# First two seven-product pairs of each FFN: own room and early loads for their weights; RMSNorm factors spread by a column

## The chip, the cores and the metric

One core of one Trainium2 chip runs the whole program. The metric is the time of one execution on the device, in microseconds (us); the median of three runs is compared.

## What is computed

One decoder layer over 520 tokens (8 tokens of running samples and a prompt of 512), model width 1024: a half-step SwiGLU FFN (hidden width 2816), a mixer (retention beside an SSD scan), cross attention over 256 memory tokens, and a second half-step FFN. Every sub-layer starts with an RMSNorm. The parts that the change touches, cut from the reference:

```python
def rmsnorm(x, gain):
    xf = x.astype(jnp.float32)
    y = xf * lax.rsqrt(jnp.mean(xf * xf, axis=-1, keepdims=True) + EPS)
    return (y * gain.astype(jnp.float32)).astype(x.dtype)

def swiglu(x, w1, w3, w2):
    return (jax.nn.silu(x @ w1) * (x @ w3)) @ w2
...
h = x + (0.5 * swiglu(rmsnorm(x, p['ffn1_norm']), p['ffn1_w1'], p['ffn1_w3'], p['ffn1_w2'])).astype(x.dtype)
```

## The kernel before

**Products.** All activations lie feature-major: 128 partitions, a tile per 128 features, 520 token columns taken as two halves of 260. Every matrix product is made in three passes on split operands (`three`: lines 472, 473, 474), hi and lo parts of weights and activations. ScalarE makes the hi part of a weight (`w_hi`, line 425 or 453), VectorE subtracts it from the loaded weight and so makes the lo part (`w_lo`, line 435). A unit is 1024 columns of weights: 8 blocks, two halves, three passes, 48 matmuls.

**The up stage of an FFN.** `w1` and `w3` have 22 pairs of tiles. The first 4 pairs (`PLAIN`) go as 8 plain units. The other 18 (`WIN`) go by a Strassen-Winograd scheme with seven products a pair: forms `a11, a12, s2, s1, s3, s4, a22`, in this order, 12 matmuls each. Their activations (`xs_hi`, `xs_lo`, from `blend`) are made by VectorE and ScalarE beside the plain units; `win_pe` waits for all four of `xs_lo` (line 766) before it starts. A pair's weights lie in five quarters of 512 columns: quarter 0 `a11`, 1 `a12`, 3 `a22`, and two sums, quarter 4 (`s1`) and quarter 2 (`s3`). A sum is made by two transfers: SyncE loads one addend, and then GpSimd's queue issues a transfer that adds the other (`sums_pool`, lines 2578 and 2579). VectorE makes two more sums from these (`s2`, `s4`: `sum_dve`, line 727), and hi and lo parts of each form are made by ScalarE (line 708) and VectorE (line 713), six forms ahead of TensorE. Even pairs use `raw_0` and `z1_0`, odd pairs `raw_1`. `raw_0` is also the buffer of the plain units' weights (`w_raw`), and `raw_1` lies over `x_hi` and `x_lo`, which the plain units read. Hence the first two pairs' loads wait:

```python
if i == 0:
    nc.sync.wait_ge(w_lo, up.u0 + up.units)
elif i == 1:
    nc.sync.wait_ge(unit_done, up.u0 + up.units)
```

The first waits until the last plain unit is split, the second until it is multiplied. SyncE's queue, like every engine's program, is strictly in order; so is VectorE's, where the places of the first forms are fixed by hand (`FIRST_FORMS`: forms 0 and 1 at plain unit 5, 2 and 3 at unit 6, 4 and 5 at unit 7). At unit 5 VectorE does form 0's lo part, the sum `s2`, form 1's lo part, and only then the output of unit 6 (line 1087) and the last `xs_lo`. After a pair's third product it adds `join` (line 827), for which TensorE waits one pair later.

**The norms.** ScalarE squares `h` and VectorE adds the squares up in `sq_sum`. `norm_rows_pe` (line 568) sums over partitions into one column per 128 tokens, ScalarE takes the root (line 582), VectorE the reciprocal (line 588) and then a diagonal matrix for each 128 tokens from it (line 590); `norm_spread_pe` (line 597) multiplies ones by these diagonals, which gives every partition the factor of every token, and ScalarE copies that to `rstd` (lines 606, 607). Outputs are scaled by `rstd` as they leave PSUM. This is done for six norms: `ffn1`, `mix`, `mem`, `ssd`, `x`, `ffn2`. In the first unit after a norm starts TensorE multiplies the not yet scaled `h`; for `ffn1` the row sums come in the middle of unit 1 and the spread after unit 1, for `mix`, `x` and `ffn2` the row sums come after unit 0 and the spread after 5 of the 8 blocks of unit 1. The third unit needs the PSUM pair of the first, which VectorE frees only with `rstd` in hand (line 1087 in an FFN, 1219 in the mixer).

## Time and profile before

| what | value |
|---|---|
| median of 3 runs | 1240.49 us (1239.48 to 1240.67) |
| the profiled execution's own time | 1237.87 us |
| its span, first to last instruction | 1236.1 us |
| TensorE busy | 1199.6 us, 97% of the span |
| VectorE busy | 794.7 us, 64% |
| ScalarE busy | 519.3 us, 42% |
| mean granted TensorE clock | 0.996 of full speed |

The profiled execution is one single run, so its span is the sum against which terms are made; it is 2.6 us below the median. TensorE's busy time counts overlapped matmuls once. A row of the timeline with x10 for five matmuls counts the two passes in which the profile shows a 4-byte product that is not split.

### The profile page before, as it was taken

What the parts mean: (1) busy time and instruction counts of PE and PEld (TensorE: products, weight loads), DVE (VectorE), ACT (ScalarE), POOL (GpSimd) and SP (SyncE); (2) the same over time, 40 slices, a digit from 0 to 9 for tenths busy, and PEclk for the clock granted to TensorE, in tenths of its full rate; (3) what the DMA queues carried; (4) which work ended last, traced back from release to release, by engine and by line L of the source; (5) the groups of instructions that cost most, each with busy time, mean ns of one, the idle gap of its engine ahead of it and who ended that gap; (6) DMA issues with size and microseconds to landing.
All of it is one profiled execution on the core that took longest, in us unless ns stands there. A gap on an engine that the chain in (4) does not pass through costs nothing.

```text
span 1236.1 us, 23510 instructions
## 1 busy us (share of the span) xinstructions
PE 1199.6 (97%) x9699; PEld 1146.0 (93%) x9699; DVE 794.7 (64%) x1246; ACT 519.3 (42%) x848; POOL 124.2 (10%) x154
## 2 busy tenths in 40 slices
PE   7999999999999999999888999999999999999997
PEld 7999999999999979999766999679999999999997
DVE  6888888863336618765787542445679888893332
ACT  6445444552223223264864421433435554562221
POOL 0012111000001000043310010200011111100000
PEclk9999999999999999999999999999999999999999
DMA  4388777343323312221575446812168777633322
GB/s 161 110 203 207 182 184 181 98 125 94 90 84 126 104 54 69 69 99 64 185 248 177 135 172 222 324 35 88 66 170 196 186 182 182 165 98 104 94 77 69
DMA packets 64212, 169.47 MB, mean 137 GB/s; under 512 B 7232, under 2 KB 9472, under 8 KB 61680
## 3 DMA queue, kind: packets, MB, share of 16 engines
q1 hardware_dynamic: 47424, 118.22, 30.5%
q0 software_dynamic: 16144, 49.29, 16.3%
q8 instruction: 74, 1.21, 0.4%
q10 hardware_dynamic: 544, 0.53, 0.1%
q14 instruction: 26, 0.21, 0.1%
HBM read 158.96 MB, written 9.06 MB: 136 GB/s over the span
## 4 chain that ended last, share of the span: by engine, by line
PE 86%; DVE 6%; ACT 3%; DMA 3%; issue 2%; SPq 0%; POOL 0%; DVEq 0%; ACTq 0%
PE ps L472 26%; PE ps L473 26%; PE ps L474 26%; DMA raw<-in_w_up 2%; PE ps L2350 1%; PE ps L2288 1%; DVE w_lo L435 1%; ACT w_hi L425 1%; ACT x_hi L613 1%; PE ps L2251 1%; PE ps L1498 1%; PE ps L597 0%; PE ps L2442 0%; DVE sq_sum L552 0%; DMA raw<-in_w_xv 0%
## 5 line engine op out<-in xcount | busy, mean ns | idle before, releaser
L472 PE MATMUL ps<-xs_lo,w_hi 128*128 128x260 f32 x1008 | 284.8, 283 | 5.2 <-DVE xs_lo L766 3.0
L473 PE MATMUL ps<-xs_hi,w_lo 128*128 128x260 f32 x1008 | 285.5, 283 | 0.0
L474 PE MATMUL ps<-xs_hi,w_hi 128*128 128x260 f32 x1008 | 284.9, 283 | 0.0
L435 DVE TENSOR_TENSOR w_lo<-raw,w_hi 128x1024 fp32r<-128x1024 f32 (+1 forms) x132 | 157.5, 1194 | 153.4 <-ACT w_hi L425 147.2
L474 PE MATMUL ps<-x_hi,w_hi 128*128 128x260 f32 (+1 forms) x896 | 253.6, 283 | 0.0
L473 PE MATMUL ps<-x_hi,w_lo 128*128 128x260 f32 (+1 forms) x896 | 253.3, 283 | 0.0
L472 PE MATMUL ps<-x_lo,w_hi 128*128 128x260 f32 (+1 forms) x832 | 241.8, 291 | 6.9 <-DVE x_lo L618 2.3
L425 ACT ACTIVATE w_hi<-raw 128x1024 fp32r<-128x1024 f32 (+1 forms) x128 | 130.8, 1026 | 208.4 <-PE ps L474 169.9
L708 ACT ACTIVATE w_hi<-raw 128x512 fp32r<-128x512 f32 x234 | 139.3, 626 | 170.2 <-DVE raw L727 135.0
L472 PE MATMUL ps<-gu_lo,w_hi 128*128 128x260 f32 x704 | 199.0, 283 | 1.6 <-DVE join L839 1.6
L472 PEld LDWEIGHTS ps<-xs_lo,w_hi 128*128 128x128 f32 x1008 | 190.0, 188 | 6.1 <-DVE xs_lo L766 3.4
L474 PEld LDWEIGHTS ps<-xs_hi,w_hi 128*128 128x128 f32 x1008 | 189.7, 188 | 0.0
L473 PEld LDWEIGHTS ps<-xs_hi,w_lo 128*128 128x128 f32 x1008 | 189.4, 188 | 0.0
L473 PEld LDWEIGHTS ps<-x_hi,w_lo 128*128 128x128 f32 x896 | 169.5, 189 | 2.0 <-issue 1.9
L474 PEld LDWEIGHTS ps<-x_hi,w_hi 128*128 128x128 f32 x896 | 169.5, 189 | 0.0
L472 PEld LDWEIGHTS ps<-x_lo,w_hi 128*128 128x128 f32 x832 | 157.5, 189 | 11.4 <-issue 10.4
L474 PE MATMUL ps<-gu_hi,w_hi 128*128 128x260 f32 x576 | 162.8, 283 | 0.0
L473 PE MATMUL ps<-gu_hi,w_lo 128*128 128x260 f32 x576 | 162.8, 283 | 0.0
L713 DVE TENSOR_TENSOR w_lo<-raw,w_hi 128x512 fp32r<-128x512 f32 x234 | 153.9, 684 | 0.8 <-ACT w_hi L708 0.7
L472 PEld LDWEIGHTS ps<-gu_lo,w_hi 128*128 128x128 f32 x704 | 132.6, 188 | 2.0 <-DVE join L839 2.0
L474 PEld LDWEIGHTS ps<-gu_hi,w_hi 128*128 128x128 f32 x576 | 108.6, 189 | 0.0
L473 PEld LDWEIGHTS ps<-gu_hi,w_lo 128*128 128x128 f32 x576 | 108.2, 188 | 0.0
(373 smaller groups left out, 1767.1 us busy)
## 6 DMA issues: line engine op xcount, KB each, us to landing
raw<-in_w_up SPq DMA_DIRECT2D x162, 256.0 KB, 3.5
raw<-in_w_down SPq DMA_DIRECT2D x32, 512.0 KB, 3.6
raw<-in_w_up POOLq DMA_DIRECT2D x54, 256.0 KB, 5.5
cache<-in_cache POOLq DMA_DIRECT2D x11, 1024.0 KB, 9.2
raw<-in_w_up SPq DMA_DIRECT2D x16, 512.0 KB, 3.5
raw<-in_w_down SPq DMA_DIRECT2D x16, 384.0 KB, 3.1
v_early<-in_cache POOLq DMA_DIRECT2D x5, 1024.0 KB, 9.8
z<-in_w_up SPq DMA_DIRECT2D x18, 256.0 KB, 2.8
```

The source lines that it names most:

```text
L425: nc.scalar.activation(w_hi_t[j][:, 0:cols], w_raw[j % RAW][:, 0:cols], ACT.Copy).then_inc(w_hi, 1)
L435: nc.vector.tensor_tensor(w_lo_t[j][:, 0:cols], w_raw[j % RAW][:, 0:cols], f32(w_hi_t[j][:, 0:cols]), ALU.subtract).then_inc(w_lo, 1)
L472: nc.tensor.matmul(out, w_h, m_l, start=start, stop=False)
L473: nc.tensor.matmul(out, w_l, m_h, start=False, stop=False)
L474: return nc.tensor.matmul(out, w_h, m_h, start=False, stop=stop)
L613: nc.scalar.activation(dest, source, ACT.Copy, scale=gain(name, k)).then_inc(x_hi_done, 1)
L708: nc.scalar.activation(form_slot(w_hi_t, n), form_source(FORMS[n]), ACT.Copy).then_inc(f_hi, 1)
L713: nc.vector.tensor_tensor(form_slot(w_lo_t, n), form_source(FORMS[n]), f32(form_slot(w_hi_t, n)), ALU.subtract).then_inc(f_lo, 1)
L1498: mm = nc.tensor.matmul(bank(6 + a), ones, ssd_au[:, a * BANK:(a + 1) * BANK], start=True, stop=True)
L2251: mm = nc.tensor.matmul(s_row(n, q), qm[:, n, d, q, :], cache[:, n % 3, (q * 2 + d) * MEM:(q * 2 + d + 1) * MEM], start=n == 0 and d == 0, ...
L2288: mm = nc.tensor.matmul(out, qx(2 * i + d)[:, chunk(c)], mem_k[:, 2 * i + d, :], start=d == 0, stop=d == 1)
L2350: mm = nc.tensor.matmul(bank(b), mem_v[:, m, n * P:(n + 1) * P], att[:, i, :], start=m == 0, stop=m == 1)
```

## The change

**Weights of the first two pairs.** `raw_first` is a new tile of five quarters for pair 1, laid over a part of `gu`'s area that nothing holds until later pairs' outputs are written. `first_win_loads` replaces the loads of pairs 0 and 1. The first addends of three sums are issued right behind the last plain unit's load (for the second FFN after a wait for the units before it); quarters 0 and 1 of pair 0 wait for the split of the last but one plain unit, quarter 2 and 3 for the split of the last, and the rest of pair 1 follows with no wait of its own. GpSimd's additions and VectorE's and ScalarE's waits for pair 0 count the first of the two additions alone where only that one is needed (`both_or_first`). Pair 2 waits for pair 0's additions and for `f_hi` of pair 0's `a22`; the wait for the last plain unit's product moves to pair 3.

**Norms.** The diagonals are gone. `spread_column` multiplies the reciprocals' column, read 128 times by its access pattern as the stationary operand, by the identity. In `ffn1` the row sums move from the middle of unit 1 to its end, so that row sums and spread stand next to each other; in `mix`, `x` and `ffn2` the spread moves from after the fifth block of unit 1 to after its second.

```diff
-        diag = sq[:, :, :].rearrange("p a c -> p (a c)")[:, 0:TOKT * P].rearrange("p (t c) -> p t c", t=TOKT)
...
-        gu, gu_lo, blend = over(FT * T, (0, "gu", [P, FT, T], F32), (0, "gu_lo", [P, FT, T], F32R),
-                                (PLAIN * T, "blend", [P, 2, 8, HT], F32), stack=ffn)
+        gu, gu_lo, blend, raw_first = over(FT * T, (0, "gu", [P, FT, T], F32), (0, "gu_lo", [P, FT, T], F32R),
+                                (PLAIN * T, "blend", [P, 2, 8, HT], F32),
+                                           (3 * PLAIN * T, "raw_first", [P, 5 * QUART], F32), stack=ffn)
...
-                if within and kk == blocks // 2:
+                if within and kk == 1:
                     within()
...
-                                  (lambda: (norm_rows_pe(norm, inv_d) if norm == "ffn1" else norm_spread_pe(norm)))
-                                  if norm and j == 1 else None).then_inc(unit_done, 1)
-                    if norm and norm != "ffn1" and j == 0:
+                                  (lambda: norm_spread_pe(norm)) if norm and norm != "ffn1" and j == 1 else None
+                                  ).then_inc(unit_done, 1)
+                    if norm and j == int(norm == "ffn1"):
                         norm_rows_pe(norm, inv_d)
                     if norm == "ffn1" and j == 1:
                         norm_spread_pe(norm)
...
-            nc.vector.reciprocal(inv, root).then_inc(diag_done, 1)
-            nc.vector.wait_ge(diag_done, 2 * r + 1)
-            nc.vector.tensor_tensor(diag[:, 0:n, :], ident.unsqueeze(1).to_broadcast([P, n, P]),
-                                    inv.unsqueeze(2).to_broadcast([P, n, P]),
-                                    ALU.mult).then_inc(diag_done, 1)
+            nc.vector.wait_ge(row_std_done, NORM_AT[name] + 1)
+            nc.vector.reciprocal(inv, root).then_inc(inv_made, 1)
+
+        def spread_column(out, inv, columns):
+
+            return nc.tensor.matmul(out, inv.to_broadcast([P, P]), ident[:, columns], start=True, stop=True)
...
-                mm = nc.tensor.matmul(ps[:, b * BANK + to:b * BANK + to + n], ones, diag[:, t, 0:n],
-                                      start=True, stop=True)
+                mm = spread_column(ps[:, b * BANK + to:b * BANK + to + n], inv[:, t:t + 1], slice(0, n))
...
         def quarter(i, q):
+            if i == 1:
+                return raw_first[:, q * QUART:(q + 1) * QUART]
...
+        def both_or_first(f, i):
+
+            return 32 * (f * (WIN // 2) + i // 2 + 1) - (16 if i == 0 else 0)
...
+        def first_win_loads(src, f, up):
+
+            one = 32 * f * (WIN // 2) + 16
+            gate, lin, gate_1, lin_1 = (src[2 * PLAIN + n] for n in range(4))
+            if f:
+                nc.sync.wait_ge(unit_done, up.u0)
+            nc.sync.dma_start(quarter(0, 4), lin[:, 0:QUART]).then_inc(z_loaded[0], 16)
+            nc.sync.dma_start(quarter(1, 4), lin_1[:, 0:QUART]).then_inc(z_loaded[1], 16)
+            nc.sync.dma_start(quarter(1, 2), gate_1[:, 0:QUART]).then_inc(z_loaded[1], 16)
+            nc.sync.wait_ge(w_lo, up.u0 + up.units - 1)
+            nc.sync.dma_start(quarter(0, 0), gate[:, 0:QUART]).then_inc(a11_loaded[0], 16)
+            nc.sync.dma_start(quarter(0, 1), gate[:, QUART:]).then_inc(rest_loaded[0], 16)
+            nc.sync.wait_ge(w_lo, up.u0 + up.units)
+            nc.sync.wait_ge(z_loaded[0], one)
+            nc.sync.dma_start(quarter(0, 2), gate[:, 0:QUART]).then_inc(z_loaded[0], 16)
+            nc.sync.wait_ge(rest_loaded[0], one)
+            nc.sync.dma_start(quarter(0, 3), lin[:, QUART:]).then_inc(rest_loaded[0], 16)
+            nc.sync.dma_start(quarter(1, 0), gate_1[:, 0:QUART]).then_inc(a11_loaded[1], 16)
+            nc.sync.dma_start(quarter(1, 1), gate_1[:, QUART:]).then_inc(rest_loaded[1], 16)
+            nc.sync.dma_start(quarter(1, 3), lin_1[:, QUART:]).then_inc(rest_loaded[1], 16)
...
+                if i == 2:
+                    nc.sync.wait_ge(z_added[0], both_or_first(f, 0) + 16)
...
-                nc.gpsimd.wait_ge(z_loaded[i % 2], 32 * (f * (WIN // 2) + i // 2 + 1))
+                nc.gpsimd.wait_ge(z_loaded[i % 2], both_or_first(f, i))
                 nc.gpsimd.dma_start(quarter(i, 4), lin[:, QUART:], accum_op=ALU.add).then_inc(z_added[i % 2], 16)
+                if i == 0:
+                    nc.gpsimd.wait_ge(z_loaded[0], both_or_first(f, 0) + 16)
+                    nc.gpsimd.wait_ge(z_added[0], both_or_first(f, 0))
                 nc.gpsimd.dma_start(quarter(i, 2), lin[:, 0:QUART], accum_op=ALU.add).then_inc(z_added[i % 2], 16)
```

**TensorE at the first norm.** In the kernel before the row sums (line 568) stand inside unit 1 (weights `w_hi1`, `w_lo1`):

```order
L473 MATMUL ps<-x_hi,w_lo1 128x260
L474 MATMUL ps<-x_hi,w_hi1 128x260
L568 MATMUL ps<-square,sq_sum 128x1 x5
L472 MATMUL ps<-x_lo,w_hi1 128x260
L473 MATMUL ps<-x_hi,w_lo1 128x260
```

and the spread (line 597) stands at unit 1's end, ahead of unit 2 (`w_hi2`):

```order
L473 MATMUL ps<-x_hi,w_lo1 128x260
L474 MATMUL ps<-x_hi,w_hi1 128x260
L597 MATMUL ps<-sq,square 128x128 x4
L597 MATMUL ps<-sq,square 128x8
L472 MATMUL ps<-x_lo,w_hi2 128x260
L473 MATMUL ps<-x_hi,w_lo2 128x260
```

After the change the same place of the program reads:

```order
L472 MATMUL ps<-x_lo,w_hi1 128x260
L473 MATMUL ps<-x_hi,w_lo1 128x260
L474 MATMUL ps<-x_hi,w_hi1 128x260
L568 MATMUL ps<-square,sq_sum 128x1 x5
L591 MATMUL ps<-square,row_std 128x128 x4
L591 MATMUL ps<-square,row_std 128x8
L472 MATMUL ps<-x_lo,w_hi2 128x260
L473 MATMUL ps<-x_hi,w_lo2 128x260
```

Unit 1 is no longer cut, and nothing but the round over ScalarE and VectorE lies between row sums and spread.

**SyncE at the start of the seven-product stage.** Before, behind the plain units' loads (`raw_0`, x6), pair 0 goes to `z1_0` and `raw_0` and pair 1 to `raw_1`:

```order
L2548 DMA raw_0<-in_w_up1 128x1024 x6
L2564 DMA z1_0<-in_w_up1 128x512
L2566 DMA raw_0<-in_w_up1 128x512
L2568 DMA raw_0<-in_w_up1 128x512
L2569 DMA raw_0<-in_w_up1 128x512
L2571 DMA raw_0<-in_w_up1 128x512
L2564 DMA raw_1<-in_w_up1 128x512
L2566 DMA raw_1<-in_w_up1 128x512
L2568 DMA raw_1<-in_w_up1 128x512
L2569 DMA raw_1<-in_w_up1 128x512
L2571 DMA raw_1<-in_w_up1 128x512
L2564 DMA z1_0<-in_w_up1 128x512
```

After the change:

```order
L2553 DMA raw_0<-in_w_up1 128x1024 x6
L2561 DMA z1_0<-in_w_up1 128x512
L2562 DMA raw_first<-in_w_up1 128x512
L2563 DMA raw_first<-in_w_up1 128x512
L2565 DMA raw_0<-in_w_up1 128x512
L2566 DMA raw_0<-in_w_up1 128x512
L2569 DMA raw_0<-in_w_up1 128x512
L2571 DMA raw_0<-in_w_up1 128x512
L2572 DMA raw_first<-in_w_up1 128x512
L2573 DMA raw_first<-in_w_up1 128x512
L2574 DMA raw_first<-in_w_up1 128x512
L2594 DMA z1_0<-in_w_up1 128x512
```

Three first addends, two of them pair 1's, now stand ahead of everything of pair 0's that needs `raw_0`, and pair 1 no longer waits for `raw_1`.

## Rows read from the trace of the kernel before

**Rows 1.** The page's part 1: busy us (share of the span) xinstructions.

```profile
PE 1199.6 (97%) x9699; PEld 1146.0 (93%) x9699; DVE 794.7 (64%) x1246; ACT 519.3 (42%) x848; POOL 124.2 (10%) x154
```

**Rows 2.** Who TensorE waited for: us in total, times, longest us.

```profile
PE ps L472 <- DVE xs_lo L766: 3.0, 2, 1.6
...
PE ps L472 <- DVE w_lo L713: 2.2, 2, 1.2
```

**Rows 3.** Timeline of TensorE, first norm: start us, us, instruction [idle before <-releaser].

```profile
20.57 1.35 PE L568 MATMUL ps<-square,sq_sum 128*128 128x1 f32 x10 [2.47 <-DVE sq_sum L552]
...
25.45 1.18 PE L597 MATMUL ps<-sq,square 128*128 128x128 f32 x10
...
28.21 0.36 PE L472 MATMUL ps<-x_lo,w_hi 128*128 128x260 f32 x1 [1.58 <-DVE sq L1087]
```

**Rows 4.** Timeline of VectorE at the first norm.

```profile
22.32 0.19 DVE L588 RECIPROCAL row_std<-row_std 128x5 f32<-128x5 f32 x1 [0.64 <-ACT row_std L582]
22.55 0.82 DVE L590 TENSOR_TENSOR sq<-square,row_std 128x640 f32<-128x640 f32 x1
```

**Rows 5.** Windows of TensorE: stretch, us, busy (xcount), granted clock, DMA share, GB/s.

```profile
20.00:26.00 6.00, 5.43 (x33) 0.72 0.27 90
26.00:30.00 4.00, 2.42 (x22) 1.00 0.00 0
```

**Rows 6.** Timeline at the mixer's norm, VectorE and TensorE.

```profile
382.43 0.19 DVE L588 RECIPROCAL row_std<-row_std 128x5 f32<-128x5 f32 x1 [3.53 <-ACT row_std L582]
...
385.62 1.18 PE L597 MATMUL ps<-sq,square 128*128 128x128 f32 x10
...
391.14 0.36 PE L472 MATMUL ps<-x_lo,w_hi 128*128 128x260 f32 x1 [2.09 <-DVE xf L1219]
```

**Rows 7.** Timeline at the memory's and the SSD's norm, VectorE and TensorE.

```profile
596.09 0.42 DVE L590 TENSOR_TENSOR sq<-square,row_std 128x256 f32<-128x256 f32 x1
...
596.57 0.71 PE L597 MATMUL ps<-sq,square 128*128 128x128 f32 x4 [0.82 <-DVE sq L590]
...
665.33 1.28 PE L597 MATMUL ps<-sq,square 128*128 128x128 f32 x10 [0.54 <-DVE sq L590]
```

**Rows 8.** Timeline at the second FFN's norm, TensorE, ScalarE and VectorE.

```profile
870.36 1.17 PE L568 MATMUL ps<-square,sq_sum 128*128 128x1 f32 x10
...
871.61 1.28 ACT L582 ACT_TABLE_LOAD   x1 [4.80 <-PE ps L568]
...
873.28 0.19 DVE L588 RECIPROCAL row_std<-row_std 128x5 f32<-128x5 f32 x1 [5.06 <-ACT row_std L582]
```

**Rows 9.** Timeline of TensorE, start of the first FFN's seven-product stage.

```profile
64.28 0.39 PE L472 MATMUL ps<-xs_lo,w_hi 128*128 128x260 f32 x1 [1.39 <-DVE xs_lo L766]
...
75.69 0.28 PE L473 MATMUL ps<-xs_hi,w_lo 128*128 128x260 f32 x1
75.81 0.28 PE L474 MATMUL ps<-xs_hi,w_hi 128*128 128x260 f32 x1
77.25 0.39 PE L472 MATMUL ps<-xs_lo,w_hi 128*128 128x260 f32 x1 [1.17 <-DVE w_lo L713]
```

**Rows 10.** Timeline of VectorE in the same stretch.

```profile
54.58 2.05 DVE L766 TENSOR_TENSOR xs_lo<-blend,xs_hi 128x1820 fp32r<-128x1820 f32 x1
...
60.36 0.69 DVE L727 TENSOR_TENSOR raw<-raw,z 128x512 f32<-128x512 f32 x1 [2.54 <-DMA raw<-in_w_up]
...
62.18 2.04 DVE L766 TENSOR_TENSOR xs_lo<-blend,xs_hi 128x1820 fp32r<-128x1820 f32 x1
...
75.30 0.69 DVE L727 TENSOR_TENSOR raw<-raw 128x512 f32<-128x512 f32 x1 [5.39 <-DMA raw<-in_w_up]
```

**Rows 11.** Timeline of the issuing queues of SyncE and GpSimd there.

```profile
50.40 0.33 SPq L2564 DMA_DIRECT2D z<-in_w_up  x1
...
62.92 0.33 SPq L2564 DMA_DIRECT2D raw<-in_w_up  x1
...
66.48 0.85 POOL L2578 DMA_DIRECT2D raw<-in_w_up  x1 [10.40 <-DMA raw<-in_w_up]
```

More of the change, by code:

```diff
@@ L408, in build @@
         row_std_done = sem("row_std_done")
-        diag_done = sem("diag_done")
+        inv_made = sem("inv_made")
         spread_done = sem("spread_done")
@@ L628, in norm_of_h_dve @@
         def norm_of_h_dve(name):
-            norm_diag_dve(name)
+            norm_inv_dve(name)
             nc.vector.wait_ge(rstd_done, NORM_AT[name] + 1)
@@ L698, in form_hi @@
             elif name in ("a12", "a22"):
-                nc.scalar.wait_ge(rest_loaded[i % 2], 32 * loads)
+                nc.scalar.wait_ge(rest_loaded[i % 2], both_or_first(f, i) if name == "a12" else 32 * loads)
             elif name in ("s1", "s3"):
-                nc.scalar.wait_ge(z_added[i % 2], 32 * loads)
+                nc.scalar.wait_ge(z_added[i % 2], both_or_first(f, i) if name == "s1" else 32 * loads)
             else:
@@ L2099, in slots @@
             put(12, "act", lambda: norm_rows_act("ssd"))
-            put(12, "dve", lambda: norm_diag_dve("ssd"))
+            put(12, "dve", lambda: norm_inv_dve("ssd"))
             put(13, "pe", lambda: norm_spread_pe("ssd", 6))
@@ L2554, in load_win @@
                 if i == 0:
-                    nc.sync.wait_ge(w_lo, up.u0 + up.units)
-                elif i == 1:
+                    first_win_loads(src, f, up)
+                if i <= 1:
+                    continue
+                if i == 3:
                     nc.sync.wait_ge(unit_done, up.u0 + up.units)
@@ L2568, in load_win @@
                 nc.sync.dma_start(quarter(i, 0), gate[:, 0:QUART]).then_inc(a11_loaded[i % 2], 16)
+                if i == 2:
+                    nc.sync.wait_ge(f_hi, f * NFORM + FORM_AT["a22", 0] + 1)
                 nc.sync.dma_start(quarter(i, 1), gate[:, QUART:]).then_inc(rest_loaded[i % 2], 16)
```

11 lines of the change are left out of this document (5 added, 6 removed).

## The prediction

> **What bounds the kernel now.** I read the page's busy shares first. TensorE is busy 97% of the span, 1199.6 us [rows 1]; the span is 1236.1 us, so all its idle time is 36 us. The change takes no matmul away: it still has row sums and spread for each norm, seven products a pair, and as many transfers. So a gain can only come out of those 36 us, or out of the time that TensorE spends at the lower clock. I then asked who TensorE waited for. Four waits are at the start of the seven-product stages of the two FFNs: 3.0 us in two waits for `xs_lo`, 2.2 us in two waits for a form's lo part [rows 2]. The waits at the norms I took from the timeline: 2.47 us and 1.58 us at the first norm [rows 3], 2.09 us at the mixer's [rows 6], 0.82 and 0.54 us at the memory's and the SSD's [rows 7]. Together that is 12.7 us, all of it in places that the change edits.
>
> One correction is needed for all of these. The timeline counts idle time from the end of a matmul's 0.28 us, but in a full stream one starts every 0.12 us [rows 9]. A wait thus costs 0.16 us more than its idle time.
>
> **Part 1, the first norm.** The row sums can't begin before 20.57 us, since they wait for `sq_sum` [rows 3]. Today TensorE is cut in the middle of unit 1 for that, and after the row sums has 18 matmuls of unit 1 left, which end at 25.45; only then comes the spread, and unit 2 starts at 28.21. From spread to unit 2 it is 2.76 us (spread, copy to `rstd`, first output off PSUM). After the change the 18 matmuls stand before the row sums and fit in the idle 2.47 us: 18 x 0.12 is 2.2 us. The row sums start at 20.57 as before, the reciprocal ends at 22.32 + 0.19 = 22.51 [rows 4], the diagonal's 0.82 us are gone, and the spread starts at about 22.57. Unit 2 starts at 22.57 + 2.76 = 25.33 in place of 28.21: 2.88 us gained. The new form of the spread has the same count of columns, and I give it the same duration; VectorE and ScalarE start their work on `rstd` as much earlier, so unit 3 and the later ones don't get a new wait from them.
>
> The clock takes some of it back. In the window from 20 to 26 us the granted clock is 0.72 of full speed, that is at 1.2 GHz for 6 x 0.28 / 0.5 = 3.4 us, and what TensorE did before was the idle 2.47 us and 1.2 us of one-column matmuls [rows 3, 5]. That slow stretch fell on the 18 matmuls (3.7 us instead of 2.2), so it is part of the 28.21. In the next window, with 1.18 us of spread and 1.58 us idle, the clock stayed at 1.00. After the change the row sums, the round to VectorE, the spread and the round to `rstd` stand together, from 20.3 to 25.33: 5 us in which TensorE does 2.4 us of small matmuls. That is more quiet than what brought the clock down before, so I expect 1.2 GHz again, now over the first 3 us of unit 2, whose matmuls take twice as long: 1.5 us lost. The bounds are nothing (no fall, or the slow time lies in the quiet stretch) and 3.4 / 2 = 1.7 us. I take 1.5, nearest to the row of the longer quiet. Net: 1.4 us.
>
> The Trainium skill says of this (TensorE: Matmul & The Clock Gate, Part 1) that a reduced clock is the default, to which idleness returns the array, and that activity releases it. The trace agrees for the longer quiet, and in the shorter one (1.58 us) shows no fall; by the rule a merged quiet speaks against the change and costs the 1.5 us, by the shorter row alone nothing is lost and the sum below is 1.5 us larger.
>
> **Part 2, the other norms.** At the mixer's norm the reciprocal is there at 382.62, and TensorE ends the second block of unit 1 at about 383.5, so the spread finds its column ready: it stands three blocks ahead of today's 385.62, and three blocks are 18 x 0.12 = 2.15 us. Behind it is the chain spread, `rstd`, rope, first output, which ends in TensorE's wait of 2.09 us plus 0.16 [rows 6]. All but 0.1 us of that wait goes: 2.15 us. At the memory's norm and the SSD's TensorE waits for the diagonal itself. The first needed 0.42 us and TensorE idled 0.82; the second stood for 0.54 us [rows 7]. The diagonal gone gives 0.42 and 0.54, about 0.95 us; the bounds are nothing (the ScalarE splits behind it wait for something else) and that. At the norm `x` no wait stands today, so nothing is gained.
>
> At the second FFN's norm there is a loss. ScalarE loads a table there only after the row sums, 1.28 us from 871.61, and the reciprocal ends at 873.28 + 0.19 = 873.47 [rows 8]. The row sums end at 870.36 + 1.17 = 871.53 and two blocks are 12 x 0.12 = 1.4 us: TensorE reaches the spread at 872.9 and waits 0.6 us for it. Five blocks covered that; two don't. What is queued behind is the whole of TensorE, so 0.6 us are lost. VectorE does get `rstd` 1.5 us sooner, which nobody waits for.
>
> **Part 3, start of the seven-product stage.** Today pair 0's first transfer is issued at 50.40, after the last plain unit is split, and five quarters come at once [rows 11]. VectorE, which ended an `xs_lo` at 56.6, stands idle for 2.54 us before the sum `s2` at 60.36, behind which are the output of unit 6 and the last `xs_lo`, from 62.18 to 64.22 [rows 10]. TensorE starts at 64.28 [rows 9]. After the change the first addend goes out behind unit 7's load, so ahead of unit 7's split that 50.40 waited for, and pair 0's quarters 0 and 1 after the split of unit 6. Then `s2` and two lo parts take 3 x 0.6 from 56.6, unit 6 (a unit is 48 x 0.12 = 5.7 us and the last ends near 62.8) is done at 57.0, so its output runs to 59.1 and `xs_lo` to 61.1. That is 1.7 us before TensorE needs it; the wait is gone.
>
> The second wait: pair 1 is issued from 62.92, GpSimd's addition at 66.48, and VectorE stands 5.39 us for it until 75.30 [rows 10, 11]; the `join` and the lo part of `a12` are behind, and TensorE waits until 77.25 [rows 9]. After the change both addends of pair 1 leave before 50.40, over 12 us sooner than at 62.92, against the 5.39 us that VectorE stood for them; this wait goes too. Both are the same in the second FFN [rows 2]. The gain is 3.0 + 2.2 us and 4 x 0.16: 5.8 us.
>
> What is late next? Pair 2. Its first addend waits for pair 0's `s1` lo part, now near 62.3, its quarter 2 for `s3`'s, near 65. Its additions go out at about 69 and, with the 8.8 us that pair 1's took between issue and use in a crowded moment [rows 10, 11], are there at 78. TensorE reaches pair 2's third product 17 x 1.43 us after 62.8, at 87. There are 8 us to spare, and the additional early transfers meet a queue that before was empty. The extra waits put in SyncE's queue (for pair 0's additions) are for things long done by then.
>
> **The sum.** 2.9 - 1.5 + 2.15 + 0.95 - 0.6 + 5.8 = 9.7 us. The profiled execution of 1237.87 us would take 1228.2; the median of the runs, 2.6 us above it, gives 1240.49 - 9.7 = 1230.8 us.
>
> **Rivals.**
> - The clock does not fall at the first norm, or falls where nothing runs: 1.5 us more, 1229.3. It is the neighbour of my forecast and lies in its range.
> - The waits at the seven-product start come back in another form: VectorE is the one that TensorE waits for in both, it is nearly full there, and if its work is late for a reason other than the transfers, only the norms' 3.9 us stay: 1236.6. Speaks for it: the order on VectorE is as before. Against: its two idle stretches of 2.54 and 5.39 us are longer than TensorE's waits. 10%.
> - The norms give nothing, since `rstd` comes early but another condition of the third unit is late, while the 0.6 us are lost: 1240.49 - 5.8 + 0.6 = 1235.3. 5%.
> - Slower: at the first norm the clock falls and does not come back for a long time, since unit 2 starts in a bad moment. A plain unit at 1.2 GHz takes 5.7 us more. Beyond the 1.5 us already counted, 9.7 us are eaten when the clock stays low for another 19.4 us, till near the end of unit 3; from there it decides, and a further 30 us at 1.2 GHz give 1240.49 - 9.7 + 15 = 1245.8. Against it: the only slow stretch inside the span before lasted 3.4 us. 2%.
> - The early transfers are no earlier in effect and the spread no sooner: no change, 1240.5. 2%.
>
> **Numbers.** My forecast with its neighbour holds 81%, alone from 1228 to 1234 (the clock's bounds 1.7 to 0, the memory's and SSD's 0.95 to 0, and a residue of a wait at the start of the seven products). The range of 1227.8 to 1235.5 takes in the norms' rival and leaves out the third case and the last two, and a little at each end. A difference of 0.2%, 2.5 us, is about what a measurement of this kernel can tell from no change. Faster by more than that: all of the first three cases but a fraction, 0.94; within: 0.04; slower: 0.02.
>
> **What would show it.** Right, if the changed kernel's profile has the first spread at 22.6 us and unit 2 at 25.3 with a slow stretch of some 3 us behind it; no wait for `xs_lo` or for a form's lo part at the start of either seven-product stage; no VectorE idle for transfers in front of `s2`; no 2 us wait at the mixer's third unit; and a wait of 0.6 us for the reciprocal's column at the second FFN. I am wrong if a new wait stands at pair 2 (transfers or `f_lo`), if the column-fed spread takes much longer than 1.2 us, or if the clock is low for more than 4 us.

## The result and the profile after

The changed kernel took 1229.74 us (median of 4 runs, 1229.04 to 1230.62), the kernel before 1240.55 us beside it (4 runs, 1239.48 to 1240.67): a ratio of 0.9917, 95% interval 0.9904 to 0.9930. The medians are 10.8 us apart. The forecast was 9.7 us less and 1230.8 us. The profiled execution took 1229.19 us (span 1227.4), against 1237.87 (span 1236.1) before: 8.7 us. These two are single executions; why their difference is 2 us smaller than that of the medians is told below.

The page's first part, busy us, share and instructions of each engine:

```profile
PE 1204.3 (98%) x9699; PEld 1150.1 (94%) x9699; DVE 791.8 (65%) x1240; ACT 521.0 (42%) x848; POOL 124.2 (10%) x154
```

TensorE has the same 9699 instructions as in [rows 1], and is busy 4.7 us longer in a span 8.7 us shorter. So 13.4 us of idle time went, and 4.7 us of busy time were added: matmuls at the lower clock. VectorE lost six instructions, the diagonals.

Who TensorE waited for (us in total, times, longest us):

```profile
PE ps L1772 <- DVE state L1751: 1.7, 1, 1.7
...
PE ps L591 <- DVE row_std L587: 1.5, 3, 0.7
...
PE ps L568 <- DVE sq_sum L552: 1.1, 2, 0.8
```

The rows for `xs_lo` and for a form's `w_lo` of [rows 2] are gone, 5.2 us of idle time. `row_std` is new: the spreads now wait for the reciprocal's column itself.

The timeline of TensorE at the five norms (start, us, instruction, [idle before]):

```profile
20.29 1.25 PE L568 MATMUL ps<-square,sq_sum 128*128 128x1 f32 x10 [0.33 <-DVE sq_sum L552]
22.19 1.28 PE L591 MATMUL ps<-square,row_std 128*128 128x128 f32 x10 [0.65 <-DVE row_std L587]
25.05 0.56 PE L472 MATMUL ps<-x_lo,w_hi 128*128 128x260 f32 x1 [1.58 <-DVE sq L1092]
...
380.01 1.18 PE L591 MATMUL ps<-square,row_std 128*128 128x128 f32 x10
...
590.49 0.71 PE L591 MATMUL ps<-square,row_std 128*128 128x128 f32 x4 [0.36 <-DVE row_std L587]
...
659.37 1.28 PE L591 MATMUL ps<-square,row_std 128*128 128x128 f32 x10
...
867.52 1.28 PE L591 MATMUL ps<-square,row_std 128*128 128x128 f32 x10 [0.45 <-DVE row_std L587]
```

At the first norm the 2.47 us of idle time are 0.33 now, since the 18 matmuls of unit 1 fill them, and unit 2 starts at 25.05 in place of 28.21 [rows 3]. The column-fed spread takes what the old one took. At the mixer's norm no wait stands where 2.09 us stood [rows 6]; at the memory's 0.36 us in place of 0.82, at the SSD's nothing in place of 0.54 [rows 7].

Windows of TensorE (stretch, us, busy of PE, PEld, DVE, ACT, POOL, granted clock, DMA share, GB/s):

```profile
20.00:26.00 6.00, 3.47 (x24) 3.36 (x25) 3.11 (x5) 4.29 (x8) 0.00 (x0) 0.86 0.31 87
26.00:30.00 4.00, 4.00 (x21) 4.00 (x20) 3.97 (x9) 2.77 (x4) 0.00 (x0) 0.50 0.44 131
30.00:32.00 2.00, 2.00 (x14) 2.00 (x14) 1.96 (x3) 1.91 (x2) 0.00 (x0) 0.71 0.11 14
...
600.00:606.00 6.00, 5.45 (x25) 4.34 (x26) 4.33 (x10) 5.21 (x14) 2.97 (x3) 0.72 0.49 163
640.00:650.00 10.00, 8.93 (x42) 6.25 (x43) 7.92 (x13) 2.32 (x5) 2.67 (x5) 0.83 0.92 340
```

A window's clock gives its time at 1.2 GHz as (1 - clock) / 0.5 of its length: 1.7 + 4.0 + 1.2 us in the first three, 6.8 us in one piece from about 24.3 to 31.2. Before it was 3.4 us, and over at 26 [rows 5]. The last two windows hold 3.4 us each; the same windows of the kernel before have a clock of 1.00.

VectorE, and then the issuing queues of SyncE and GpSimd, at the start of the first seven-product stage:

```profile
55.63 0.69 DVE L732 TENSOR_TENSOR raw<-raw,z 128x512 f32<-128x512 f32 x1
...
57.45 2.04 DVE L771 TENSOR_TENSOR xs_lo<-blend,xs_hi 128x1820 fp32r<-128x1820 f32 x1
```

```profile
36.64 1.91 SPq L2561 DMA_DIRECT2D z<-in_w_up  x1
38.59 0.43 SPq L2562 DMA_DIRECT2D raw_first<-in_w_up  x1
...
48.70 0.33 SPq L2569 DMA_DIRECT2D raw<-in_w_up  x1
...
51.83 0.85 POOL L2614 DMA_DIRECT2D raw<-in_w_up  x1 [9.13 <-DMA raw<-in_w_up]
52.37 1.19 POOL L2610 DMA_DIRECT2D raw_first<-in_w_up  x1
...
67.56 0.85 POOL L2610 DMA_DIRECT2D z<-in_w_up  x1 [13.12 <-DMA raw<-in_w_up]
```

SyncE's three first addends leave at 36.6 to 39.5 us, 11 and more before pair 0's first load in [rows 11]. GpSimd's additions for pair 1 leave at 52.37 and after, behind pair 0's second one, and not before 50.40 as the prediction has it of both addends; that is still 14.1 us sooner than the 66.48 of [rows 11]. VectorE makes the sum `s2` at 55.63 without a wait (before: 60.36, after 2.54 us), and the last `xs_lo` ends at 59.5 (before: 64.2) [rows 10]. TensorE's first matmul of the stage starts at 62.33 and stands in a stream without a gap.

**Where the time went.** How far the changed kernel runs ahead, from starts of the same TensorE instruction in both timelines (us):

| place | before | after | ahead | step |
|---|---|---|---|---|
| first matmul | 8.49 | 8.21 | 0.28 | no cause in the change |
| unit 2 of the first stage | 28.21 | 25.05 | 3.16 | +2.88 |
| last matmul of the plain units | 62.61 | 62.21 | 0.40 | -2.76 |
| first of the seven products | 64.28 | 62.33 | 1.95 | +1.55 |
| end of that stage | 247.38 | 243.91 | 3.47 | +1.52 |
| third unit at the mixer's norm | 391.14 | 385.53 | 5.61 | +2.15 |
| memory's spread | 596.57 | 590.49 | 6.08 | +0.47 |
| SSD's spread | 665.33 | 659.37 | 5.96 | -0.12 |
| attention | 745.61 | 739.62 | 5.99 | 0 |
| seven products of the second FFN | 914.56 | 907.52 | 7.04 | -0.73 +1.78 |
| end (last matmul) | 1229.31 | 1220.79 | 8.52 | +1.48 |

### The profile page after: what moved, and what is told of

It is laid out like the page before. It is cut to its first block, busy times and chain, and to the rows that moved or that the text cites. A ratio compares the mean times of both kernels' runs of the same rounds, so it can differ in the third digit from the quotient of the medians.

```text
span 1227.4 us, 23512 instructions
## 1 busy us (share of the span) xinstructions
PE 1204.3 (98%) x9699; PEld 1150.1 (94%) x9699; DVE 791.8 (65%) x1240; ACT 521.0 (42%) x848; POOL 124.2 (10%) x154
## 4 chain that ended last, share of the span: by engine, by line
PE 91%; DVE 4%; ACT 3%; issue 1%; DMA 0%; DVEq 0%; SPq 0%; ACTq 0%
PE ps L472 28%; PE ps L473 27%; PE ps L474 27%; PE ps L2355 1%; PE ps L2293 1%; DVE w_lo L435 1%; ACT x_hi L612 1%; PE ps L2256 1%; PE ps L1503 1%; PE ps L591 1%; PE ps L2447 0%; ACT w_hi L425 0%; DMA h<-in_xT 0%; PE ps L568 0%; DVE sq_sum L552 0%
## 5 line engine op out<-in xcount | busy, mean ns | idle before, releaser
L713 ACT ACTIVATE w_hi<-raw 128x512 fp32r<-128x512 f32 x220 | 131.8, 627 | 152.0 <-DVE raw L732 117.7
L718 DVE TENSOR_TENSOR w_lo<-raw,w_hi 128x512 fp32r<-128x512 f32 x220 | 145.0, 684 | 0.1
```

Source lines behind the costliest of these rows:

```text
L713: nc.scalar.activation(form_slot(w_hi_t, n), form_source(FORMS[n]), ACT.Copy).then_inc(f_hi, 1)
L718: nc.vector.tensor_tensor(form_slot(w_lo_t, n), form_source(FORMS[n]), f32(form_slot(w_hi_t, n)), ALU.subtract).then_inc(f_lo, 1)
```

## The experiments

Each is named by what is in it. The kernel before was timed beside them: 1240.5 us beside e1 to e4 (17 runs), 1240.47 beside e5 to e8 (27 runs), 1240.27 beside e9 to e11 (23 runs). The bracket behind a ratio is its 95% interval.

**e1, the norm edits alone**: the column, the sums and the spreads at their new places; all loads as before.

```diff
-                if within and kk == blocks // 2:
+                if within and kk == 1:
...
-                    if norm and norm != "ffn1" and j == 0:
+                    if norm and j == int(norm == "ffn1"):
...
-            norm_diag_dve(name)
+            norm_inv_dve(name)
```

> The kernel before with the norms' half of the change alone (column spread, moved row sums and spreads; the weights of the first two pairs as before). If the two halves are independent sums of removed waits, the four waits at the starts of the seven-product stages are all back (their total in the trace before, start to start, is 1.55 + 1.32 + 1.78 + 1.22, about 6 us), and it runs 6 us above the changed kernel, near 1235.8. Rival: the norms' earlier factors already give VectorE the time it lacked there, so some of these waits are gone without the early loads: under 1233. Second rival: the norms' gain is eaten by the clock, and it stays within 2 us of before.

Measured 1237.25 us (12 runs, 1233.21 to 1240.48), ratio 0.9974 (0.9963 to 0.9985): 3.25 us less.

**e2, the load edits alone**: the other hunks of the change.

```diff
+                                           (3 * PLAIN * T, "raw_first", [P, 5 * QUART], F32), stack=ffn)
...
+                    first_win_loads(src, f, up)
+                if i <= 1:
+                    continue
```

> The kernel before with the weights' half alone. Independent halves: the four waits are gone and nothing else, 6 us below before, near 1234.5, and the trace has no wait for xs_lo or a form's lo part at either stage's start. Rival: the early transfers only work because the norm's part moved SyncE's and VectorE's work ahead too: less than 3 us gained.

Measured 1232.86 us (6 runs, 1231.44 to 1234.82), ratio 0.9937 (0.9921 to 0.9954): 7.6 us less. Its trace has no wait for `xs_lo` or for a form's lo part at the start of either stage. The halves add up: 3.25 + 7.6 is 10.9 us, the whole change 10.8. That they need each other, or cover the same time, is not borne out; by the two intervals (1.9 to 4.6 and 5.7 to 9.8 us) an overlap of a few us can't be excluded by the times alone. The loads gave 1.8 us more than the 5.8 that I reckoned for the four waits, the norms 0.65 us less than 3.9.

**e9, the column alone**: no diagonals, but sums and spreads where they were.

```diff
-            nc.vector.tensor_tensor(diag[:, 0:n, :], ident.unsqueeze(1).to_broadcast([P, n, P]),
-                                    inv.unsqueeze(2).to_broadcast([P, n, P]),
-                                    ALU.mult).then_inc(diag_done, 1)
...
+            return nc.tensor.matmul(out, inv.to_broadcast([P, P]), ident[:, columns], start=True, stop=True)
```

> This is the kernel before with one edit alone: the norms are spread from the reciprocal's column, without the diagonal matrices, while the row sums and the spreads stay at their old places in the unit order and all loads are as before. In the rows of the kernel before, the diagonal stood on TensorE's path at two norms only: 0.47 us at the memory's and 0.5 to 0.6 us at the SSD's. At the first norm the sums are asked for so early before the spread that only the chain sum, root, diagonal, spread counts there: 0.8 us for the diagonal's product. If the price of the diagonal is what I take it for: about 1.0 us less at the two norms, and 0.8 us at the first and 0.8 at the mixer norm where the spread follows the sums by one unit only if that unit is the shorter one, so 1237.9 to 1239.5 us, most likely 1239.3. Rival: the moves of the sums and spreads did nothing and the column does all of the 3.25 us that the norm edits gave together: 1237.2 us. Rival: the diagonal lay beside other work everywhere: 1240.5 us. Against it works the scatter of the four waits at the seven-product pairs, which is as large as what is looked for.

Measured 1238.85 us (12 runs, 1236.44 to 1240.72), ratio 0.9984 (0.9973 to 0.9994): 1.4 us less, 0.7 to 3.3 by the interval. Unit 2 of the first stage still starts at 28.20: there the diagonal was hidden by the 18 matmuls. The wait at the mixer's third unit stands as before:

```profile
391.85 0.56 PE L471 MATMUL ps<-x_lo,w_hi 128*128 128x260 f32 x1 [2.10 <-DVE xf L1217]
```

In e1 unit 2 starts at 25.30 and that wait is gone. So by the traces the column gives what was TensorE's wait for the diagonal at the memory's and the SSD's norm, and the moved sums and spreads give the rest. The medians of e9 and e1 are 1.6 us apart, less than their scatter (4.3 and 7.3 us over 12 runs each), and don't show it by themselves.

**e3, the change with filler matmuls** around the first spread: one ahead of it and three behind, on data that is there, into a free bank (the trace records each as two, x2 and x6).

```diff
                     if norm == "ffn1" and j == 1:
+                        keep_busy(1)
                         norm_spread_pe(norm)
+                        keep_busy(3)
```

> The changed kernel with four matmuls of 260 columns that nobody reads in the idle time around the first norm's spread, one before it and three after it. Theory: the quiet stretch there brings the clock down, and the slow stretch behind it costs the 2.8 us that unit 2 and its followers took longer in the changed kernel's trace. Then the clock stays at full speed and the median falls by 2 to 3 us, to about 1227. Rival: the slow stretch has another cause or is made up for later: no change, 1229.7, or, when the fillers delay unit 2, up to 0.5 us more.

Measured 1226.23 us (4 runs, 1225.82 to 1226.62), ratio 0.9881 (0.9863 to 0.9900): 3.5 us less than the change. TensorE's timeline and windows of it:

```profile
21.42 0.69 PE L537 MATMUL ps<-h 128*128 128x260 f32 x2
22.20 1.28 PE L597 MATMUL ps<-square,row_std 128*128 128x128 f32 x10
23.34 1.56 PE L537 MATMUL ps<-h 128*128 128x260 f32 x6
25.06 0.36 PE L472 MATMUL ps<-x_lo,w_hi 128*128 128x260 f32 x1 [0.16 <-DVE sq L1098]
```

```profile
20.00:26.00 6.00, 5.43 (x37) 4.55 (x37) 3.11 (x5) 4.29 (x8) 0.00 (x0) 1.00 0.24 87
26.00:30.00 4.00, 4.00 (x36) 4.00 (x35) 3.96 (x9) 2.77 (x4) 0.00 (x0) 1.00 0.44 131
```

Unit 2 starts at 25.06, as in the changed kernel (25.05), but at a clock of 1.00: 36 matmuls in the window from 26 to 30 against 21. The useful work is the same and begins at the same time, so the quiet stretch around the first spread is shown to be what brings the clock down. Its price is 3.5 us by the medians and 2.6 us by the two profiled executions (1229.19 and 1226.62).

**e5, the kernel before with such fillers**, five before the row sums and three behind the spread.

```diff
+            keep_busy(5)
+            norm_rows_pe(norm, inv_d)
...
                         norm_spread_pe(norm)
+                        keep_busy(3)
```

> The kernel before with eight matmuls of 260 columns that nobody reads: five ahead of the first norm's row sums, where TensorE idles 2.47 us, and three behind its spread. Theory: the slow clock was in the kernel before too and cost the 1.5 us by which the 18 matmuls behind the row sums took longer (3.7 us for 2.2), so about 1.5 us less, 1239. Rival: it was hidden there, or fillers delay the row sums by as much: no change.

Measured 1239.0 us (11 runs, 1238.39 to 1242.09), ratio 0.9991 (0.9982 to 1.0001), not told apart from no change. In its profile unit 2 does start 1.5 us sooner, and at full clock:

```profile
26.72 0.36 PE L472 MATMUL ps<-x_lo,w_hi 128*128 128x260 f32 x1 [0.16 <-DVE sq L1096]
...
63.94 0.39 PE L472 MATMUL ps<-xs_lo,w_hi 128*128 128x260 f32 x1 [2.55 <-DVE xs_lo L775]
```

The first of the seven products starts at 63.94, 0.34 us sooner than in [rows 9], after a wait of 2.55 us instead of 1.39. TensorE came sooner, the transfers did not: in this profile 1.2 of the 1.5 us went into the wait. Time won ahead of 62 us can be lost there as long as the loads are late.

**e4, the second FFN's spread after its fifth block** rather than after the second; otherwise the change.

```diff
-                if within and kk == 1:
+                if within and kk == at:
...
+                                  at=4 if norm == "ffn2" else 1)
```

> The changed kernel with the second FFN's spread put back behind the fifth block. Theory: TensorE's wait for the reciprocal's column there (0.45 us idle, 0.6 us from start to start) is gone and nothing takes its place: 0.6 us less, 1229.1, which may be too small to be told in the median but shows in the trace. Rival: the factors come 1.5 us later and VectorE is late for the seven products again: a wait at xs_lo, 1230 or more.

Measured 1228.2 us (4 runs, 1228.0 to 1228.69), ratio 0.9899 (0.9881 to 0.9918), 1.5 us less than the change, with no wait at that spread. That is more than the 0.7 us that the wait cost from start to start. Its four executions have a mean granted clock of 0.993 to 0.995, those of the change 0.991 and 0.992, and its profile lacks the slow stretch at 643 us, which this edit does not touch; so about 0.7 us are the edit's and I don't put down the rest to it.

**e8, e3 with the square root's table loaded early** for the second FFN as well.

```diff
-            if name == "ffn1":
+            if name in ("ffn1", "ffn2"):
                 spare = row_std[
```

> The changed kernel with the four fillers around the first norm's spread and with ScalarE's table for the root of the second FFN's norm loaded ahead of its wait for the row sums. Theory: both remaining losses of the change go, 2.8 us and 0.6 us: about 1226.3, below both kernels. Rival: as for the fillers alone, no change from the first; the table load then gives at most 0.6 us.

Measured 1225.63 us (4 runs, 1224.97 to 1227.42), ratio 0.9874 (0.9859 to 0.9889), the lowest median: 4.1 us less than the change and 14.8 less than before. It is 0.6 us below e3, whose runs (1225.82 to 1226.62) lie inside e8's (1224.97 to 1227.42), so the times don't show that the table's part gains anything; the trace shows that its wait is gone. ScalarE's timeline:

```profile
859.82 1.28 ACT L586 ACT_TABLE_LOAD   x1
...
864.56 0.27 ACT L588 ACTIVATE row_std<-ps,square 128x5 f32<-128x5 f32 x1 [3.25 <-PE ps L574]
```

The load is over 3.5 us before the root is taken, where in [rows 8] it stood behind the row sums, and no wait stands at the spread. The Trainium skill (ScalarE: Activation LUTs, What ACT_TABLE_LOAD costs) has a price of about 1283 ns for such a load; the trace agrees with 1.28 us.

**e6, pair 1's own room without the early addends**: pair 1 no longer waits for the last plain product, but all ten quarters leave after the last plain unit is split. With the norm edits; the diff is to e1, whose `quarter` also gets the two lines for `raw_first`.

```diff
-                elif i == 1:
+                elif i == 3:
                     nc.sync.wait_ge(unit_done, up.u0 + up.units)
```

> Norms as changed; pair 1 has its own room, but all loads are issued after the last plain unit is split, pair 0's first and pair 1's behind them with no wait for the last plain unit's product. Theory: two separate waits with two causes. The wait for xs_lo is back (its cause is pair 0's sum, issued at the same time as before: 1.55 + 1.78 us), the wait for the lo part of pair 1's a12 is gone: 3.3 us above the changed kernel, about 1233. Rival: both waits hang on when the first addend leaves, and both are back: about 1235.8, as with the norms alone. Or pair 1's transfers crowd pair 0's and the first wait is longer than before.

Measured 1241.73 us (11 runs, 1239.58 to 1243.66), ratio 1.0010 (1.0000 to 1.0019): a miss by nearly 9 us. TensorE's waits, VectorE's sum and the windows:

```profile
65.46 0.39 PE L472 MATMUL ps<-xs_lo,w_hi 128*128 128x260 f32 x1 [3.81 <-DVE xs_lo L767]
...
917.17 0.58 PE L472 MATMUL ps<-xs_lo,w_hi 128*128 128x260 f32 x1 [4.55 <-DVE xs_lo L767]
```

```profile
61.54 0.69 DVE L728 TENSOR_TENSOR raw<-raw,z 128x512 f32<-128x512 f32 x1 [6.86 <-DMA raw<-in_w_up]
```

```profile
50.00:55.00 5.00, 5.00 (x44) 5.00 (x43) 4.58 (x6) 2.36 (x2) 1.89 (x2) 1.00 0.93 277
55.00:60.00 5.00, 5.00 (x44) 5.00 (x43) 0.00 (x0) 0.63 (x1) 1.73 (x2) 1.00 1.06 279
```

The second pair's waits are gone, as meant, but the first pair's are 3.8 and 4.6 us and not 1.4 and 1.6. VectorE gets pair 0's quarter 1.2 us later than in [rows 10], though the loads left from 47.85 us on, 2.5 us earlier. My theory then: pair 1's five transfers, issued right behind pair 0's, share the DMA engines with pair 0's additions, which are issued last and needed first.

**e10, e6 with one wait**: pair 1's loads leave when pair 0's additions have landed.

```diff
+                elif i == 1:
+                    nc.sync.wait_ge(z_added[0], 32 * (f * (WIN // 2) + 1))
                 elif i == 3:
```

> The kernel with pair 1's own room and pair 0's loads as late as before (1241.7 us), with one wait more: pair 1's five loads are issued only when pair 0's additions have landed, near 60 us instead of 49 to 52. Theory (pair 1's transfers crowd pair 0's additions, and that made the first pair's waits 3.8 and 4.6 us): the first pair's waits fall back to what the kernel before has, 1.4 to 3 us, VectorE's first idle time for pair 0's sum ends near 60 instead of 61.5 us, pair 1 still comes early enough for no wait of its own, or one under 1 us, and the time is about 1235.8 us (1237.25 of the norms alone, less most of the second pair's waits), 1234 to 1237.5. Rival (the place in gu's area costs by itself, or the pair that comes first waits for something else than its additions): the waits of 3.8 and 4.6 us stay, and so does the time, 1241 to 1242 us. Rival (the spacing only moves the wait to pair 1): no wait over 3 us at pair 0, one of 2 to 4 us at pair 1, 1237 to 1240 us.

Measured 1232.8 us (6 runs, 1230.79 to 1233.31), ratio 0.9937 (0.9924 to 0.9951): 8.9 us less than e6 by a wait added to a queue, and 3 us below what I expected.

```profile
62.66 0.39 PE L472 MATMUL ps<-xs_lo,w_hi 128*128 128x260 f32 x1 [0.39 <-DVE xs_lo L767]
...
909.08 0.39 PE L472 MATMUL ps<-xs_lo,w_hi 128*128 128x260 f32 x1 [1.46 <-DVE xs_lo L767]
```

```profile
58.74 0.69 DVE L728 TENSOR_TENSOR raw<-raw,z 128x512 f32<-128x512 f32 x1 [3.43 <-DMA raw<-in_w_up]
```

```profile
55.00:60.00 5.00, 5.00 (x44) 5.00 (x44) 1.57 (x4) 0.34 (x1) 0.00 (x0) 1.00 0.54 92
```

Pair 0's sum comes 2.8 us sooner than in e6, and the two waits are 0.39 and 1.46 us. Crowding is shown to be the cause of the long waits. These are 6.5 of the 10.9 us by which the two profiled spans differ (1239.9 and 1229.0 us); the rest goes with the clock, low for 20.5 us in e6's profile (added up over the windows of the whole trace, 3.4 and 6.8 us of it behind the two waits) and for 6.8 us in e10's.

**e7, early addends without own room**: pair 0 as in the change, pair 1 into the old buffer after the last plain product.

```diff
-            if i == 1:
-                return raw_first[:, q * QUART:(q + 1) * QUART]
...
-            nc.sync.dma_start(quarter(1, 4), lin_1[:, 0:QUART]).then_inc(z_loaded[1], 16)
-            nc.sync.dma_start(quarter(1, 2), gate_1[:, 0:QUART]).then_inc(z_loaded[1], 16)
...
+            nc.sync.wait_ge(unit_done, up.u0 + up.units)
+            nc.sync.dma_start(quarter(1, 4), lin_1[:, 0:QUART]).then_inc(z_loaded[1], 16)
+            nc.sync.dma_start(quarter(1, 2), gate_1[:, 0:QUART]).then_inc(z_loaded[1], 16)
```

> Norms as changed; pair 0 is loaded early as in the change, pair 1 lies in raw_1 as before and waits for the last plain unit's product. Theory: the wait for xs_lo is gone, the one for the lo part of a12 is back (1.32 + 1.22 us): 2.5 us above the changed kernel, 1232.3. Rival: pair 1's transfers now meet an idle queue, since pair 0's are long done, and its sum is in time: 1229.7.

Measured 1241.7 us (11 runs, 1240.27 to 1242.61), ratio 1.0006 (0.9997 to 1.0015), again a miss, by 9.4 us.

```profile
77.85 0.59 PE L472 MATMUL ps<-xs_lo,w_hi 128*128 128x260 f32 x1 [4.20 <-DVE w_lo L716]
...
929.13 0.39 PE L472 MATMUL ps<-xs_lo,w_hi 128*128 128x260 f32 x1 [3.91 <-DVE w_lo L716]
```

```profile
70.00:75.00 5.00, 3.65 (x31) 3.45 (x29) 0.00 (x0) 0.00 (x0) 1.73 (x2) 1.00 1.07 266
75.00:80.00 5.00, 2.15 (x10) 2.15 (x11) 4.07 (x8) 1.67 (x3) 0.00 (x0) 0.68 0.53 97
```

No wait stands at pair 0. TensorE starts the stage sooner and stands longer for pair 1, whose loads can't leave before 62 us; and pair 2's loads, free to go once pair 0's forms are split, leave right behind them (64.56 us in the trace). The second window shows the clock fallen behind the wait of 4.20 us.

**e11, e7 with one wait**: pair 2's loads leave when pair 1's additions have landed.

```diff
                 if i == 2:
                     nc.sync.wait_ge(z_added[0], both_or_first(f, 0) + 16)
+                    nc.sync.wait_ge(z_added[1], both_or_first(f, 1))
```

> The kernel with pair 0's early loads and addends, and pair 1 in its old room (1241.7 us), with one wait more: pair 2's loads are issued only when pair 1's additions have landed, so not right behind pair 1's. Theory (pair 2's transfers crowd pair 1's, and that made the second pair's waits 4.2 and 3.9 us rather than the 2.2 to 3.2 us of a pair 1 that is loaded at the same place alone): the second pair's waits fall to 2.2 to 3.2 us, the slow stretches behind them get shorter or go, and the time is 1237 to 1239 us. Pair 2's own additions then come some 8 us later than in that kernel, and it had about as much to spare: a wait at pair 2 up to 1.5 us in each FFN would show there and give 1240 us. Rival (the wait is the old room's distance from its last reader alone, and pair 2 does nothing to it): 4.2 and 3.9 us stay, 1241 to 1242.5 us.

Measured 1238.31 us (12 runs, 1237.11 to 1241.33), ratio 0.9990 (0.9979 to 1.0000): 3.4 us less than e7, as the theory had it.

```profile
74.42 0.39 PE L472 MATMUL ps<-xs_lo,w_hi 128*128 128x260 f32 x1 [0.56 <-DVE w_lo L716]
...
86.63 0.39 PE L472 MATMUL ps<-xs_lo,w_hi 128*128 128x260 f32 x1 [1.81 <-DVE w_lo L716]
...
926.62 0.39 PE L472 MATMUL ps<-xs_lo,w_hi 128*128 128x260 f32 x1 [1.50 <-DVE w_lo L716]
...
938.53 0.39 PE L472 MATMUL ps<-xs_lo,w_hi 128*128 128x260 f32 x1 [1.51 <-DVE w_lo L716]
```

Pair 1's waits fall to 0.56 and 1.50 us, further than to the 2.2 that I gave as the theory's lower end, and pair 2 pays with 1.81 and 1.51. That is the price of the spacing when the room is missing: what is needed is both that pair 1 can leave early and that nothing is put in front of what is needed first.

## Why the prediction was right, point by point

**The first norm, before the clock: right.** Forecast: the spread from 28.21 - 2.76 to 22.57, unit 2 earlier by 2.88 us. Measured: earlier by 2.88 us once the start of the program is set equal. The spread was reached at 22.19 + 0.28 = 22.47.

**The clock, right in kind, mis-sized.** I took 1.5 us, with 1.7 as the upper bound. It cost 2.76. The step that failed is the length of the slow stretch: I took the 3.4 us of [rows 5] for the length of any such stretch, and it was 6.8. About 6.1 us of the stretch lie behind unit 2's start at 25.05, and there a matmul starts every 0.217 us instead of 0.12: 6.1 x 0.45 is 2.7 us. The same length stands in the profiles of e4, e7, e10 and e11, 3.4 us in those of e1 and e6, so it differs between executions. In e7, e10 and e11 it begins earlier, so that the spread itself is slow:

```profile
22.37 2.08 PE L591 MATMUL ps<-square,row_std 128*128 128x128 f32 x10 [0.65 <-DVE row_std L587]
```

That row is of e10, and unit 2 starts at 26.04 there instead of 25.05. Net, the first norm's edits gave 2.88 - 2.76 = 0.1 us in the changed kernel's profile, where 1.4 us were forecast: in this profile the part is worth next to nothing without fillers.

My sign that the prediction is wrong, a clock that is low for more than 4 us, was met; the total was right because of what follows. The rival without any fall (1229.3) did not happen: the window from 26 to 30 us has 0.50, and e3, where the fillers keep the clock up, is at 1226.2.

**The mixer's norm**: 2.15 us forecast, 2.15 measured. **The memory's and the SSD's**: 0.95 forecast; 0.47 at the first, and at the second the waits of the row sums and of the spread went, 0.5 and 0.6 us from start to start. Between the two stand terms that I did not have: two slow stretches, which cost about 1.6 us each, and two waits for `state` (0.99 and 0.91 us in the profile of before) that are missing behind them, since TensorE gets there later. So 0.35 us came of the 0.95. The slow stretches are not the change's: e2, where no norm is edited, has such stretches at 605 and 660 us, and e10, with the norms edited, has neither and has the `state` wait back.

**The second FFN's norm**: a loss, as forecast, of 0.73 us from start to start instead of 0.6, with 0.45 us of idle time before the spread. In e8's trace that wait is gone, since the table is loaded earlier.

**The seven products**: four waits for 5.8 us; the table has 1.55 + 1.52 + 1.78 + 1.48 = 6.3 us. A wait costs about 0.1 us more than its idle time and the 0.16 us that I added: behind the wait at 64.28 in the kernel before, the second matmul starts 0.22 us after the first and not 0.12.

**The total.** In the two profiled executions my sum of 9.7 us came out as 8.2: 1.3 less for the clock at the first norm, 0.6 less between the memory's norm and the SSD's, 0.1 less at the second FFN's, 0.5 more at the waits (and 0.28 us at the program's start, in no term). The norms' terms alone are 1.9 us there, where 3.9 were forecast. The medians differ by 10.8. What I had done was to subtract the sum for the profiled execution of the kernel before from the median of its runs, as if both had the same clock. They have not. Over the 67 executions of the kernel before that were timed beside these kernels, the mean granted clock goes from 0.989 to 0.997 and the time from 1243.6 to 1236.9 us with it (correlation -0.81, slope 0.74 us for each 0.001). The profiled one, with 0.996, is among the best; the median has 0.993, so 2.2 us more by the slope. That matches the 2 us by which the medians differ more than the two profiled executions. So the total was right in part by luck: this and the terms that came out too large cancelled to 1.1 us.

Where a usual execution of the kernel before has its additional slow stretches is only partly seen. The profiles of e2 and e5, whose norms are those of before, each have two in the memory's part (from 604 and 658 us, from 608 and 662), and that of e9 one behind the mixer's wait of 2.10 us (granted clock 0.72 from 390 to 396), where the profiles of before, e2 and e5 stay at 1.00. With the old loads, one of the four waits can be 3.2 us or nothing, though their sums are alike (idle time of 5.0, 5.4 and 5.0 us in the profiles of e1, e5 and e9, 5.2 in [rows 2]); behind the 2.55 us in e5, the 3.18 us in e1 and the 3.8 to 4.6 us of e6 and e7 the clock is low, as it is behind one wait of 1.76 us in e9 and one of 1.81 us in e11, while behind the other waits of 1.6 to 1.9 us in e9, e1 and e5 it stays at 1.00. The medians of the mean clock are in line with that: 0.993 before, 0.9945 with the load edits alone (e2), 0.992 with the norm edits alone (e1), 0.9915 for the change, 0.989 and 0.988 for e6 and e7, 0.996 for e3. By the slope, 1.1 of e2's 7.6 us are clock. A profile of a median execution of the kernel before was not taken, so this stays an argument from clocks, and the slope is a correlation.

**What's late next: pair 2.** No wait stands there: its additions are issued at 67.56, 1.4 us sooner than the 69 that I reckoned. The place where it would be late is wrong in the prediction, though: VectorE makes a pair's sum before the lo part of its `a12`, so TensorE would stand at that form, 15 forms of 1.43 us behind the start, near 84 us and not 87. e11 shows both: there the wait of 1.81 us stands at 86.63, with the additions issued at 76.36, 8.8 us later than in the change. So the room is about 7 us by these two numbers (an estimate), where 8 were reckoned.

**The rivals.** The return of the waits in another form (1236.6) is ruled out: no such wait stands in the changed kernel's profile, and VectorE no longer idles ahead of `s2`. In e6 and e7, each with about one half of the load edit, the waits do come back, at 3.8 to 4.6 us, and the time is that of before; but their cause is the transfers, which is not what that rival named. In the sum, and in what I expected of e6 and e7, the two early loads were independent gains of 3.0 and 2.2 us. They are not: added to e1's norms alone (1237.25 us), each half by itself costs 4.5 us, and both together gain 7.5. The norms that give nothing (1235.3) are ruled out by e1, the clock that stays low by the windows, which are back at full speed from 31.2 us.

**Left open.** Why the slow stretches in the memory's part (600 to 660 us) fall in some executions and not in others; how much of e4's 1.5 us is the moved spread; and what the median loses when the first norm's edits are left out and the others stay, which no run here tries.

## What to carry to other kernels

When a wait for transfers is taken away by issuing them earlier, ask what was until then held back by the same late issue, and put what is needed last behind the arrival of what is needed first: e10 won 8.9 us over e6 with one more wait in a queue. When small waits are merged into one quiet stretch of TensorE, price the clock as a term of its own, by more than the one slow stretch that the trace shows (here 6.8 us came where 3.4 had been seen), and try a few filler matmuls in it. Look at how the clock of the profiled execution stands among all timed ones before its waits are taken as those of the median.

## What the runs showed of the hardware

- The slow stretch at the same quiet place lasted 3.4 us in two profiles (e1, e6) and 6.8 us in five (the change, e4, e7, e10, e11); in three of these it had begun before the spread was over. The Trainium skill (TensorE: Matmul & The Clock Gate, Part 1) says that the ramp varies from run to run of one kernel; these rows fit that, though each is of another kernel with the same quiet place.
- Four matmuls, 2.2 us of TensorE's time in a place where it had to wait anyway, kept the clock at 1.00 in e3 and gave 3.5 us.
- A wait of 1.6 to 2.1 us had a slow stretch behind it in some profiles (1.76 and 2.10 us in e9, 1.81 us in e11) and none in others (1.69 us in e9, 1.85 us in e1, 2.09 us in e2).
- Ten 256 KB transfers in a row filled the DMA engines for ten us (share 0.93 and 1.06, 277 and 279 GB/s), and the two additions among them came late enough to hold up VectorE until 61.54 us; with the last five held back the share fell to 0.54 after 55 us and it went on at 58.74.
- The kernel before scatters by 6.7 us over 67 executions (1236.9 to 1243.6) and e1, with the same loads, by 7.3 over 12. The changed kernel and e4 scatter by 1.6 and 0.7 us over four each, but so did four executions of the kernel before, by 1.2 us, so that the change steadies the time is not shown.
